# Attention by pairs: DVE's first stages and ACT's exponentials of two heads in a row, and TensorE's transposes one slot behind

## The reference

```
o_a   = banded_attention(aq, ak, av, window 128, bias, sinks)   # 8 heads, softmax with a sink
o_cmp = softmax(q @ kcmp.T * scale, valid) @ vcmp               # compressed keys, 63 of them
o_slc = attention over selected blocks of 64 (16 of 16)         # so: causal attention over all keys
o_win = banded_attention(bq, bkw, bvw, window 512, bias_b)
o_b   = gates[0] * o_cmp + gates[1] * o_slc + gates[2] * o_win
g_a, g_b = split(sigmoid(mg))                                   # mg = xn @ w_in[:, 2072:]
merged = g_a * (o_a @ w_br_a) + g_b * (o_b @ w_br_b)
```

## Time and profile before

| | us |
|---|---|
| median of 3 runs | 1781.21 |
| lowest | 1778.41 |
| highest | 9073.13 |
| profiled execution, own time | 1784.23 |
| profiled execution, span | 1782.4 |
| TensorE busy in the span | 1557.8 |
| DVE busy | 537.1 |
| ACT busy | 348.3 |
| POOL busy | 262.8 |

### The profile page before, as it was taken

One profiled execution on the slowest core, in us unless ns is written; L12 is line 12 of the kernel. 1 busy time (PEld: TensorE's weight loads), 2 busy tenths in 40 slices (PEclk: granted clock), 3 DMA queues, 4 the chain that ended last, 5 costly groups with the idle time before them and its releaser, 6 DMA issues.

```text
span 1782.4 us, 20856 instructions
## 1 busy us (share of the span) xinstructions
PE 1557.8 (87%) x7526; PEld 828.0 (46%) x7527; DVE 537.1 (30%) x1378; ACT 348.3 (20%) x859; POOL 262.8 (15%) x363
## 2 busy tenths in 40 slices
PE   6999998989989898988999994199799999889990
PEld 3554543434444444443444552156355666446650
DVE  4210005665565545553222215011011111101116
ACT  3000003343433433342000111011011111111112
POOL 2000002333232232221000000300000000000003
PEclk9999999999999999998999997599899999999995
DMA  9124602443111111002536410979999999999967
GB/s 254 26 59 57 132 0 100 166 142 95 30 33 34 30 24 42 25 18 77 204 115 232 172 53 18 341 283 380 383 389 384 379 391 381 391 390 383 381 223 283
DMA packets 130215, 334.21 MB, mean 188 GB/s; under 512 B 36792, under 2 KB 72664, under 8 KB 120944
## 3 DMA queue, kind: packets, MB, share of 16 engines
q1 hardware_dynamic: 112208, 291.88, 46.8%
q0 software_dynamic: 9552, 29.55, 5.0%
q10 hardware_dynamic: 8400, 12.07, 1.9%
HBM read 276.06 MB, written 57.41 MB: 187 GB/s over the span
## 4 chain that ended last, share of the span: by engine, by line
PE 71%; DMA 9%; DVE 8%; SPq 6%; issue 3%; ACT 2%; POOL 2%; ACTq 0%; POOLq 0%; DVEq 0%
PE PS L741 13%; PE PS L642 10%; PE PS L531 10%; PE PS L755 7%; PE PS L704 6%; PE PS L673 5%; SPq L301 5%; PE PS L628 4%; PE PS L589 4%; PE PS L608 3%; PE PS L526 2%; DMA BA<-w 2%; DMA WA<-w 2%; DMA BA<-rows_d 2%; DVE mx L1022 1%
## 5 line engine op out<-in xcount | busy, mean ns | idle before, releaser
L642 PE MATMUL PS<-WA 128*128 128x512 f32 x512 | 260.3, 621 | 17.8 <-ACT WA L833 17.8
L741 PE MATMUL PS<-WA,BA 128*64 128x256 f32 x2048 | 235.8, 388 | 14.1 <-DMA WA<-w 12.9
L741 PEld LDWEIGHTS PS<-WA,BA 128*64 128x64 f32 x2048 | 172.9, 140 | 84.6 <-issue 22.1
L531 PE MATMUL PS<-WA,BA 128*128 128x512 f32 x416 | 183.1, 601 | 5.1 <-DVE WA L937 5.1
L1248 POOL TENSOR_SCALAR BA<-BA,rin,gates 128x640 f32<-128x640 f32 (+7 forms) x128 | 99.8, 780 | 301.8 <-DVE rin L1045 301.7
L1161 DVE SCALAR_TENSOR_TENSOR BA<-BA,PS 128x256 f32<-128x256 f32 x46 | 19.4, 421 | 408.4 <-ACT BA L880 408.4
L642 PEld LDWEIGHTS PS<-WA 128*128 128x128 f32 x512 | 85.6, 191 | 111.5 <-issue 80.9
L826 ACT ACTIVATE BA<-PS,ngm 128x640 f32<-128x640 f32 (+7 forms) x128 | 89.7, 701 | 218.2 <-DVE ngm L1023 218.0
L531 PEld LDWEIGHTS PS<-WA,BA 128*128 128x128 f32 x416 | 79.6, 193 | 103.9 <-issue 98.3
L755 PE MATMUL PS<-WA,BA 128*64 128x512 f32 x512 | 116.9, 597 | 11.7 <-DVE BA L1171 7.6
L1287 POOL DMA_DIRECT2D BA<-rows_d x92 | 48.1, 522 | 531.1 <-PE PS L722 528.1
(11 more groups left out here) (207 smaller groups left out, 1361.4 us busy)
## 6 DMA issues: line engine op xcount, KB each, us to landing
WA<-w SPq DMA_DIRECT2D x66, 2048.0 KB, 34.4
BA<-w SPq DMA_DIRECT2D x30, 2048.0 KB, 36.7
rows_d<-WA SPq DMA_DIRECT2D x7, 2048.0 KB, 7.5
BA<-rows_d POOLq DMA_DIRECT2D x94, 128.0 KB, 7.2
rows_d<-BA ACTq DMA_DIRECT2D x92, 128.0 KB, 7.8
WA<-w_in SPq DMA_DIRECT2D x16, 512.0 KB, 5.5
gates_d<-WA SPq DMA_DIRECT2D x32, 256.0 KB, 2.2
WA<-gates_d SPq DMA_DIRECT2D x8, 1024.0 KB, 6.0
```

Of the source, the lines that this page charges most:

```text
L531: mm = pe.matmul(PS[:, j % 4, :], ws[:, c % 6, k, :], hnT[:, k, 512 * h:512 * h + 512], start=(k == 0), stop=(k == KT - 1))
L642: mm = pe.matmul(PS[:, 6, :], gw[:, j, k, :], hnT[:, k, 512 * hf:512 * hf + 512], start=(k == 0), stop=(k == KT - 1))
L741: mm = pe.matmul(PS[DH * h:DH * h + DH, bank, 0:256], xT[:, k, :], w[par][:, k, 256 * h:256 * h + 256], start=(k == 0), stop=(k == KT - 1))
```

## The change

A list of slots is built: a slot is one A unit, one C unit, or a pair of W or S units. Each engine walks over slots instead of units. In a pair's slot DVE does both first stages, then the second stage of the first head, the copies of the prior slot's first unit, the second stage of the second head, the copies of the prior slot's second unit. ACT does both exponentials, then copies, then the tanh. TensorE makes the scores, the first unit's gate steps, the transposes of the prior slot's first unit, values that are due, the second unit's gate steps, the transposes of the prior slot's second unit. In the slot of a single unit the second stage and the transposes of the unit before come one unit closer. The planner no longer lets the first unit of a pair take a tile's last step (`opens`).

The bodies of `exponential`, `gate_tiles`, `move_groups` (ACT) and `take_groups` (DVE) are the old loops' bodies, made functions of a unit.

```diff
@@ -222,6 +222,14 @@
     pv_order = [(i, br) for i in range(TT) for br in "ACWS"]
+    slots = []
+    for u, (i, br, h, kbs) in enumerate(units):
+        second = br in "WS" and h >= REP
+        if second:
+            slots[-1].append(u)
+        else:
+            slots.append([u])
+    NS = len(slots)
 
@@ -236,7 +244,8 @@
         here = []
-        while step_no < want and (not here or step_no % KT or n == NU - 5):
+        opens = u[1] in "WS" and u[2] < REP
+        while step_no < want and (not here or step_no % KT or n == NU - 5) and not (opens and step_no % KT == KT - 1):
             here.append(step_no)
@@ -644,16 +653,24 @@
-        for n in range(NU + 3):
-            if n < NU:
-                if units[n][1] in "AC" or units[n][2] < REP:
-                    scores(n)
-                for step in steps_at[n]:
+        for s in range(NS + 2):
+            now = slots[s] if s < NS else []
+            before = slots[s - 1] if 1 <= s <= NS else []
+            if now:
+                scores(now[0])
+                for step in steps_at[now[0]]:
                     gate_step(step)
-            if 2 <= n < NU + 2:
-                turn(n - 2)
-            if n >= 3 and (n - 3) == last_of[units[n - 3][:2]]:
-                values(*units[n - 3][:2])
+            if before:
+                turn(before[0])
+            if s >= 2:
+                u = slots[s - 2][-1]
+                if u == last_of[units[u][:2]]:
+                    values(*units[u][:2])
+            for u in now[1:]:
+                for step in steps_at[u]:
+                    gate_step(step)
+            for u in before[1:]:
+                turn(u)
...
@@ -804,46 +821,63 @@
+        for s in range(NS + 2):
+            now = slots[s] if s < NS else []
+            before = slots[s - 1] if 1 <= s <= NS else []
+            for u in now:
+                exponential(u)
+            if before:
+                move_groups(before[0])
+            if s >= 2:
...
                     nc.scalar.copy(dst, PS[:, 7, :].rearrange("p (r t) -> p r t", r=REP)) \
                         .then_inc(S["o_evac"], 1)
+            for u in now:
+                gate_tiles(u)
+            for u in before[1:]:
+                move_groups(u)
 
@@ -1045,19 +1079,29 @@
-        for n in range(NU + 2):
-            if n < NU:
-                front(n)
-            if 1 <= n < NU + 1:
-                back(n - 1)
-            if n >= 2:
-                for m in range(first_group[n - 2], first_group[n - 1]):
...
+        for s in range(NS + 1):
+            now = slots[s] if s < NS else []
+            before = slots[s - 1] if s >= 1 else []
+            for u in now:
+                front(u)
+            if now:
+                back(now[0])
+            if before:
+                take_groups(before[0])
+            for u in now[1:]:
+                back(u)
+            for u in before[1:]:
+                take_groups(u)
```

More of the change, by code:

```diff
@@ new lines, in exponential @@
+        def exponential(n):
+            i, br, h, kbs = units[n]
+            act.wait_ge(S["front"], n + 1)
+            if n >= 3:
+                act.wait_ge(S["t_done"], first_group[n - 2])
+            nk = P * len(kbs)
+            s0, v = 2 * (n % 2), n % 4
+            if br == "A":
+                nc.scalar.activation(esk[:, v, :], esk[:, v, :], ACT.Exp)
+                for g in range(2):
+                    last = nc.scalar.activation(PB[:, n % 3, nk * g:nk * g + nk], PS[:, s0 + g, 0:nk],
+                                                ACT.Exp, bias=ngm[:, v, g:g + 1], scale=SC,
+                                                accum_out=den[:, v, g:g + 1])
+            elif br == "C":
+                last = nc.scalar.activation(pc[:, :, :], pc[:, :, :], ACT.Exp, scale=SC)
+            else:
+                src = PS[:, s0:s0 + 2, :].rearrange("p a n -> p (a n)")[:, 0:nk]
+                last = nc.scalar.activation(PB[:, n % 3, 0:nk], src, ACT.Exp, bias=ngm[:, v, 0:1], scale=SC,
+                                            accum_out=den[:, v, 0:1])
+            last.then_inc(S["exp_done"], 1)
@@ new lines, in gate_tiles, with move_groups @@
+        def gate_tiles(n):
+            for m in tile_done_at.get(n, ()):
+                act.wait_ge(S["gate_in"], m + 1)
+                if m >= 2:
+                    act.wait_ge(S[f"gst{m % 2}"], 16 * (m // 2))
+                nc.scalar.activation(gst[:, m % 2, :], PS[:, 6, :], ACT.Tanh, scale=0.5).then_inc(S["gate_act"], 1)
+        def move_groups(u):
+            for m in range(first_group[u], first_group[u + 1]):
+                if m % 2 == 0:
+                    move_group(m)
+        for s in range(NS + 2):
[6 more added lines that the diff above has]
+            if s >= 2:
+                u = slots[s - 2][-1]
+                i, br = units[u][:2]
+                if u == last_of[(i, br)] and br in "AS":
@@ L1045, in back, with take_groups @@
                 dve.reciprocal(rin[:, v, 0:1], den[:, v, 0:1]).then_inc(S["back"], 1)
-        for n in range(NU + 2):
-            if n < NU:
-                front(n)
-            if 1 <= n < NU + 1:
-                back(n - 1)
-            if n >= 2:
-                for m in range(first_group[n - 2], first_group[n - 1]):
-                    if m % 2 == 1:
-                        dve.wait_ge(S["t_done"], m + 1)
-                        slot_free(dve, m)
-                        for dst, src in group_copies(m):
-                            last = dve.tensor_copy(dst, src)
-                        last.then_inc(S["evac_dve"], 1)
+        def take_groups(u):
+            for m in range(first_group[u], first_group[u + 1]):
+                if m % 2 == 1:
+                    dve.wait_ge(S["t_done"], m + 1)
+                    slot_free(dve, m)
+                    for dst, src in group_copies(m):
+                        last = dve.tensor_copy(dst, src)
+                    last.then_inc(S["evac_dve"], 1)
+        for s in range(NS + 1):
[11 more added lines that the diff above has]
+                take_groups(u)
         for pi in range(2 * KT):
```

32 lines of the change are left out of this document (removed).

## The result

| | before | after |
|---|---|---|
| median, us | 1779.81 (4 runs) | 1805.47 (4 runs) |
| lowest and highest | 1777.58, 9073.13 | 1802.31, 1807.06 |
| profiled execution, own time | 1784.23 | 1806.97 |
| attention loop, from first scores to first merge matmul | 571.3 | 596.3 |
| A/C stretches in it, sum of eight | 142.8 | 174.2 |

The ratio is 1.0146, interval 1.0122 to 1.017: **25.7 us slower**, where +10.8 was forecast. In the profiled executions the loop is 25.0 us longer and 2.3 us come back behind it.

What follows compares the result with a forecast made beforehand. TensorE was taken as the bound, with about 58 us of idle time to win in the 571.3 us loop. Terms of +25.7 and −14.9 gave net +10.8 on 1784.2, 1795 us profiled or 1792 as median; range 1770 to 1816.

Steps and rivals of the forecast that it cites:

- rival (c): A/C stretches: the clock falls twice in each of eight, costing 27 us; +38 in all, 1819 us; chance 0.12.
- The price of one drop: Rival (c)'s cost of one clock fall to a mean of 0.66 over 5 us: 1.7 us.
- term 2: Pairs in the loop: back-to-back first stages save waits, limited by copies and uneven gate steps; −14.9 us.
- The slots of 6.8 us: Pair slots of blocks 5 and 7: at least 6.8 us, as ACT's bank-freeing copy queues behind both exponentials.
- Term 1: A and C units: DVE stands still for the exponential between its two stages, lengthening eight stretches; +25.7 us.
- "It adds nothing": A/C stretches: POOL's scaling is ready 5.95 us after the scores, inside the sum, so it costs no extra time.
- the list of signs: Expected in the new profile, among others: TensorE waiting for POOL's scaling in every A/C stretch.
- (a): Pairs win more: waits for exponential and tanh go, the bank frees in time; −10, 1771 us; chance 0.2.
- (b): Pairs win nothing, TensorE's order there being in effect unchanged; only term 1 is left, +26, 1807 us; chance 0.15.

Runs made afterwards that it cites:

- Fill: The changed kernel with transposes repeated in ten pair slots of blocks 5 to 7 that have few gate steps; 1794.61 us.
- its control: The changed kernel with about as many repeated transposes, but in slots of blocks 5 to 7 with many gate steps; 1821.67 us.
- Pe_old_singles: The changed kernel with single units' transposes and copies back at two units behind, DVE's new order kept; 1800.64 us.
- pairs_old: The changed kernel with pairs and planner as before, so only A and C units are changed; 1794.20 us.
- opens_alone: The kernel before the change with only the planner's rule added; 1786.48 us.
- copy_first: The changed kernel with ACT's copy for the prior pair's first unit between the two exponentials instead of behind both; 1787.42 us.
- Copy_first plus the old single units: The changed kernel with ACT's copy ahead of the second exponential and A and C units at their old lag; 1766.41 us.
- best_fill: Old-lag A and C units and ACT's copy ahead of the second exponential, plus repeated transposes in five idle slots; 1763.92 us.

## Why the prediction was right and wrong

**The step that failed: the net sum has no term for the clock.** The time lies within the stated range, but the change is 25.7 us where the sum had 10.8, and 12.0 of the 25.0 us in the loop are the clock. The sum was built from durations at full clock and priced the clock only in rival (c), as all or nothing and only for A/C stretches. The price of one drop was right: 614 to 619 us at 0.66 is the 1.7 us taken from the earlier trace rows. The number was not.

**What the runs showed in its place.** 24.2 us are 14 such drops, 12.2 are 7, and the sum had taken the seven of before as if they stayed. Of the 14, seven begin within 1.6 us of the end of one of the eight waits for ACT's copy (1.9 to 4.5 us long), the very wait that term 2 had found: six in the pairs of blocks 5 and 7, one in the A/C stretch of block 6. The others stand near waits for DVE's copy, POOL's scaling, the tanh and the C unit's exponential. The slots of 6.8 us were worked out, but not what a TensorE standing still in them does to the next one.

Fill and its control show that the idle time in those slots is cause and not company: work put into it gives 9.9 us back, the same work elsewhere costs 17.7. The Trainium skill (TensorE: Matmul & The Clock Gate, section "HAM oscillation — how this bites in real kernels") has the rule that gaps between groups of matmuls make the next group start cold. The pairs of block 5 agree (1.00 before, 0.93 after, 1.00 when filled); the A/C stretch of block 5, with waits of up to 1.7 us, kept 1.00, and block 0's stood at 0.78 in one kernel and at 1.00 in another with the same instructions there, so what sets off each single drop isn't settled here.

**Its own tests.** The prediction said it would be wrong if the clock over the loop was under 0.96; the window shows 0.96, down from 0.98, so this sign stands on its very bound and decides nothing. The other two signs of being wrong didn't come: the A/C stretches are longer, and the pair slots didn't fall to TensorE's own work.

**Term 1, +25.7.** The A/C stretches grew by 31.3 us (174.15 less 142.84), without clock loss by 22.6. In block 5: 22.90 against a forecast of 23.2; block 7, without its 1.6 us of clock, 25.7 against 26.0, and 25.69 at 1.00 in fill. "It adds nothing" of POOL's scaling was off by little in time, but as a wait it is there, 17.9 us in 16 places, as the list of signs had said. Pe_old_singles splits the 29.3 us between 144.9 and 174.2 in these stretches into 18.5 for the place of the transposes and 10.8 for DVE's order, but the first part holds work moved over from the pairs and the clock of these stretches; in the whole kernel it is 3.8 and 13.3 us. So DVE's order is the larger cost, as the term said.

**Term 2, −14.9.** Without clock loss the pairs fell by 9.6 us (406.7 against 416.3). Block 5 slot by slot, forecast then measured: 5.8, 5.8; 9.4, 9.44; 6.8, 7.2; 7.7, 9.03; 6.95, 7.04; 12.6, 14.43; 7.1, 7.82; 9.0, 10.09; the sum 65.4, 70.85. The first two agree within 0.05. Of the 5.5 us that the sum missed, 5.0 are clock loss, and they lie in the slots that missed: the fifth stood at 1.00 and missed by 0.1, the fourth and the sixth at 0.86 and 0.88 and missed by 1.3 and 1.8. Block 7 is the other miss: without clock loss its pairs grew by 4.9 us (79.7 against 74.9), where the sum had −0.1. The split between the terms was not a clean one, as pairs_old showed: single units alone cost 14.8 without clock loss, pairs and rule alone 1.8. The −14.9 rested on the forecast that uneven steps cost little; opens_alone says +7.7 on the old order, while on the new one the rule saves 17.5.

**The sum of both, without the clock: +13.0 against +10.8.** The mechanism (DVE's chain in single units; copies behind two exponentials) was right. That its own size came within 2.2 us is in part luck: term 1 was 3.1 us too large and term 2 saw 5.3 too much gain, in opposite directions. Of the rivals, (a) needed the bank to come free in time and needs copy_first and the old single units to come true. (b) had nearly the measured number, +26, but by chance: it had the pairs win nothing and term 1 alone left, and what was measured is +31.3 in A/C stretches and −6.3 in pairs. (c) had the right cause and much of the place: the clock fell in four of the eight A/C stretches, five drops where it had sixteen, and stood for 8.7 of the 12.0 us of increase; the drops in the pairs of block 5 it didn't have.

**The other sign.** Copy_first plus the old single units is the version in which the pairs pay: the wait for the copy, 23.5 us in the change, is 10.5 there, and 5.1 with the few repeats of best_fill.

**Open:** which condition sets off a single drop of the clock; the part of a clock loss that lies in idle time anyway (it isn't additive to the last us); and the best version without the planner's rule, which wasn't run.

## What to carry to other kernels

On an engine that works in order, a copy that frees a bank for the busiest engine goes ahead of the second long operation, not behind it: moving one copy in front of one exponential was worth 20.5 us. A unit that stands alone needs the distance of one unit between its first and second stage; closing it is only free where another unit's work fills the gap. When a sum of waits on TensorE changes, count each new wait of 2 to 4.5 us once as itself and once more as the clock behind it (here 1.7 us, behind seven of eight), and look for it in the granted clock of short windows. And take the clock of several executions before a difference of a few us is put down to it.
